# Expert stage of an MoE layer: gather for four experts at a time from a split token-major h

## What is computed

```python
scores = jax.nn.sigmoid((h @ w_router).astype(f32))
...
def expert_block(args):
    e, tok, wr = args
    xb = h[tok]
    y = (jax.nn.silu(xb @ w_gate[e]) * (xb @ w_up[e])) @ w_down[e]
    return y * wr[:, None].astype(h.dtype)
...
shared = (jax.nn.silu(h @ ws_gate) * (h @ ws_up)) @ ws_down
return routed + shared
...
h <- LayerNorm(alpha * h + moe(h))
```

## Time and profile before

| | |
|---|---|
| time, median of 3 runs | 2540.41 us (2539.84 to 2541.12) |
| span of the profiled execution | 2540.7 us, mean granted clock of PE 0.986 |
| PE busy | 2418.9 us (95%) |
| PEld busy | 1855.8 us (73%) |
| DVE busy | 1187.0 us (47%) |
| ACT busy | 676.3 us (27%) |
| POOL busy | 39.4 us (2%) |
| DMA | 635.25 MB, mean 250 GB/s |
| chain that ended last | PE 88%; DVE 8%; issue 2% |

### The profile page before, as it was taken

How to read it: one execution, slowest core, us unless ns; L and a number is a source line. 1 busy time by engine, 2 the same in 40 slices (tenths; PEclk the granted TensorE clock), 3 DMA queues, 4 the chain that set the end, 5 groups by cost and what they waited for, 6 DMA issues and landing times.

```text
span 2540.7 us, 41313 instructions
## 1 busy us (share of the span) xinstructions
PE 2418.9 (95%) x16502; PEld 1855.8 (73%) x16502; DVE 1187.0 (47%) x1447; ACT 676.3 (27%) x719; POOL 39.4 (2%) x36
## 2 busy tenths in 40 slices
PE   6999999999989999999987999999999999999995
PEld 6999999998989999999987544455444445444542
DVE  4346665757654444444456333333233333333335
ACT  3333433333333333333322111111111111111111
POOL 0000000001010000000000000000000000000000
PEclk9999999999999999999998999999999999999998
DMA  4544444443445555555762788898888889888882
GB/s 186 183 160 148 158 144 147 146 162 117 150 160 177 185 186 183 180 185 182 287 252 83 323 361 360 361 380 371 361 359 360 360 367 385 359 361 361 359 361 93
DMA packets 89095, 635.25 MB, mean 250 GB/s; under 512 B 10416, under 2 KB 10544, under 8 KB 12224
## 3 DMA queue, kind: packets, MB, share of 16 engines
q1 hardware_dynamic: 85680, 616.82, 62.0%
q10 hardware_dynamic: 2304, 10.49, 1.0%
q0 software_dynamic: 1040, 6.85, 0.7%
HBM read 632.02 MB, written 2.10 MB: 250 GB/s over the span
## 4 chain that ended last, share of the span: by engine, by line
PE 88%; DVE 8%; issue 2%; ACT 1%; DMA 0%; DVEq 0%; ACTq 0%; SPq 0%
PE bank L240 44%; PE bank L740 17%; PE bank L713 10%; PE bank L763 9%; PE bank L725 4%; PE bank L451 3%; DVE acc L1469 3%; DVE wlo L1007 1%; PE bank L410 1%; ACT whi L784 1%; DVE cv L1103 0%; DMA raw<-units 0%; DVE bns L1324 0%; PE bank L755 0%; DVE ylo L1264 0%
## 5 line engine op out<-in xcount | busy, mean ns | idle before, releaser
L1007 DVE TENSOR_TENSOR wlo<-raw,whi 128x2048 fp32r<-128x2048 f32 x206 | 477.3, 2318 | 460.7 <-ACT whi L784 458.7
L240 PE MATMUL bank<-xhi,whi 128*128 128x256 f32 x1920 | 551.7, 287 | 8.0 <-DVE wlo L1007 8.0
L240 PE MATMUL bank<-xlo,whi 128*128 128x256 f32 x1920 | 544.3, 284 | 0.0
L240 PE MATMUL bank<-xhi,wlo 128*128 128x256 f32 x1920 | 544.3, 283 | 0.0
L784 ACT ACTIVATE whi<-raw 128x2048 fp32r<-128x2048 f32 x204 | 389.6, 1910 | 438.3 <-PE bank L240 438.3
L740 PE MATMUL bank<-wgu,xg 128*64 128x512 f32 x2048 | 445.0, 592 | 1.1 <-DVE xg L1461 1.1
L240 PEld LDWEIGHTS bank<-xhi,whi 128*128 128x128 f32 x1920 | 369.5, 192 | 11.2 <-DVE wlo L1007 9.1
L240 PEld LDWEIGHTS bank<-xlo,whi 128*128 128x128 f32 x1920 | 369.6, 193 | 2.1 <-issue 1.9
L240 PEld LDWEIGHTS bank<-xhi,wlo 128*128 128x128 f32 x1920 | 369.5, 192 | 0.0
L740 PEld LDWEIGHTS bank<-wgu,xg 128*64 128x64 f32 x2048 | 148.0, 137 | 292.2 <-issue 292.2
L713 PEld LDWEIGHTS bank<-pick,h 128*128 128x128 f32 x2112 | 240.8, 194 | 30.5 <-issue 30.5
(11 more groups left out here) (322 smaller groups left out, 2814.8 us busy)
## 6 DMA issues: line engine op xcount, KB each, us to landing
wgu<-wgu SPq DMA_DIRECT2D x248, 1024.0 KB, 14.5
raw<-units SPq DMA_DIRECT2D x210, 1024.0 KB, 4.8
wd<-wd SPq DMA_DIRECT2D x128, 1024.0 KB, 8.6
wgu<-wgu ACTq DMA_DIRECT2D x8, 1024.0 KB, 9.3
h<-xtok POOLq DMA_DIRECT2D x2, 1024.0 KB, 7.0
ln_gain<-lnp POOLq DMA_DIRECT2D x2, 1024.0 KB, 13.0
ln_bias<-lnp POOLq DMA_DIRECT2D x2, 1024.0 KB, 17.9
out<-acc SPq DMA_DIRECT2D x4, 512.0 KB, 2.6
```

What stands on the lines that cost most here:

```text
L240: m = nc.tensor.matmul(out_bank[:, t * UC:(t + 1) * UC], lhsT, rhs, start=first and t == 0 and k == 0 and j == 0, stop=last and k == UK - ...
L1007: V.tensor_tensor(wlo[u % SPLIT][:, :], raw[u % RAW][:, :], whi[u % SPLIT][:, :].bitcast(f32), ALU.subtract).then_inc(lo_done, 1)
```

## The change

`htok` is split, once, into `tok_hi` (ACT, two copies of 128x2048) and `tok_lo` (POOL, two subtractions of 128x2048, written over `htok`). ACT makes ALPHA times h first, straight into `acc`, so that DVE's start of `acc` becomes a plain addition. `pick` now covers four experts (a quad): 128 x 2 x 256, type fp32r. A gather block makes two column blocks of h for four experts, hi and lo, as eight fp32r matmuls with 256 moving columns; eight such blocks make a quad. `xg` is 16 KB wide and doubled, and four blocks for the next quad are done in each pair. They stand between the scatter's parts: block, two chunks, three times, the transposes of `eact`, block, two chunks. The down product uses banks 4, 5, 0 and 1. The loop is unrolled over four pairs. `acc` becomes two tiles, and most small tiles move. Gain and bias of the second LayerNorm are loaded by SP behind the last gate and up product.

DVE does `choose` for a quad and `weigh` (the former pickw pair) at the end of the pair's code; PE waits for `pick_ok` ahead of the gate and up products of each even pair (`half == 0`).

The diff, cut to its core (`...` marks what is left out; ACT's loop mirrors DVE's):

```diff
+QUADS = PAIRS // 2
+Q4 = 4 * CAP
...
-    acc = at("acc", 128, [P, TT, D])
-
-    EP = E + 4
+    acc = [at("acc0", 32, [P, D]), at("acc1", 192, [P, D])]
+    tok_hi = at("h_tok_hi", 128, [P, TT, D], f32r)
+    tok_lo = at("h_tok_lo", 144, [P, TT, D], f32r)
+
+    EP = E + 8
...
-    xg = at("xg", 32, [P, KT, 2 * CAP])
-    pick = at("pick", 56, [P, TT, 2, CAP])
-    pickw = at("pickw", 57, [P, TT, 2, CAP])
+    xg = [at(f"xg{j}", 40 + 16 * j, [P, KT, Q4]) for j in range(2)]
+    pick = at("pick", 200, [P, TT, 4, CAP], f32r)
+    pickw = at("pickw", 202, [P, TT, 2, CAP])
...
+        sp.wait_ge(ex["gu_free"], n_rounds * (4 * PAIRS) + START)
+        sp.dma_start(lng[1][:, :], lnp[2].partition_broadcast(P)).then_inc(ex["g2"], 16)
+        sp.dma_start(lnb[1][:, :], lnp[3].partition_broadcast(P)).then_inc(ex["g2"], 16)
         for t in range(TT):
...
-        pool.wait_ge(unit_used, N_UNITS - N_X)
-        pool.dma_start(lng[1][:, :], lnp[2].partition_broadcast(P)).then_inc(ex["g2"], 16)
-        pool.dma_start(lnb[1][:, :], lnp[3].partition_broadcast(P)).then_inc(ex["g2"], 16)
+        for t in range(TT):
+            pool.wait_ge(tk["alpha_ok"], TT)
+            pool.wait_ge(tk["hi_ok"], t + 1)
+            nc.gpsimd.tensor_tensor(tok_lo[:, t, :], htok[:, t, :], tok_hi[:, t, :].bitcast(f32), ALU.subtract)\
+                .then_inc(tk["lo_ok"], 1)
...
+            pe.wait_ge(tk["lo_ok"], TT)
+
+            def gather_block(i, j, before):
+
+                pe.wait_ge(ex[("xg_act", "xg_dve")[j % 2]], b * (2 * PAIRS + 4) + before + START)
+                for k in range(2):
+                    o = bank[j % 2][:, k * Q4:(k + 1) * Q4]
+                    sl = slice((2 * i + k) * P, (2 * i + k + 1) * P)
+                    for t in range(TT):
+                        for x, h in enumerate((tok_hi, tok_lo)):
+                            mi = nc.tensor.matmul(o, h[:, t, sl], pick[:, t, :, :].rearrange("p j s -> p (j s)"),
+                                                  start=t == 0 and x == 0, stop=t == TT - 1 and x == 1)
+                mi.then_inc(ex["ga_ps"], 1)
...
+                for j in chunks:
+                    t, c = j // 4, j % 4
+                    pe.wait_ge(ex["acc_ok"], b * (8 * PAIRS + 8) + i * 8 + max(0, j - 1) + START)
...
+            pe.wait_ge(ex["pick_ok"], b * (QUADS + 2) + 1)
+            for j in range(8):
+                gather_block(j, j, j // 2)
+            with pe.Fori(0, PAIRS // 4) as four:
+                for u in range(4):
+                    pair = four * 4 + u
+                    it = b * PAIRS + pair
+                    buf, half = xg[u // 2], u % 2
...
+                    if half == 0:
+                        pe.wait_ge(ex["xg_act"], b * (2 * PAIRS + 4) + (pair * 2 + 4) + START)
+                        pe.wait_ge(ex["xg_dve"], b * (2 * PAIRS + 4) + (pair * 2 + 4) + START)
+                        pe.wait_ge(ex["pick_ok"], b * (QUADS + 2) + (four * 2 + (u // 2 + 2)))
+                    pe.wait_ge(ex["a_ok"], it + START)
                     for c in range(4):
...
-            gather(0)
-            with pe.Fori(0, PAIRS) as pair:
-                it = b * PAIRS + pair
-
-                pe.wait_ge(ex["xg_act"], b * (2 * PAIRS + 2) + (pair * 2 + 2) + START)
-                pe.wait_ge(ex["xg_dve"], b * (2 * PAIRS + 2) + (pair * 2 + 2) + START)
-                pe.wait_ge(ex["a_ok"], it + START)
-                for c in range(4):
...
-                gather(pair + 1)
-                pe.wait_ge(ex["a_ok"], it + 1 + START)
-                pe.wait_ge(ex["pt_ok"], it + START)
...
-                pe.wait_ge(ex["y_split"], it * 4 + START)
-                scatter(pair)
-                pe.wait_ge(ex["pickw_ok"], it + 1)
-                pe.wait_ge(ex["at_ok"], it + 1)
...
-                for c in range(4):
-                    pe.wait_ge(ex["y_split"], it * 4 + max(0, c - 1) + START)
...
+                    pe.wait_ge(ex["zero"], b * 3 + 3)
+                    pe.wait_ge(ex["y_split"], it * 4 + START)
+                    pe.wait_ge(ex["pt_ok"], it + START)
+                    for j in range(3):
+                        gather_block(4 * half + j, j, pair * 2 + (4 + j // 2))
+                        scatter(pair, (2 * j, 2 * j + 1))
+                    pe.wait_ge(ex["a_ok"], it + 1 + START)
...
+                    gather_block(4 * half + 3, 3, pair * 2 + 5)
+                    scatter(pair, (6, 7))
+
+                    pe.wait_ge(ex["at_ok"], it + 1)
+                    pe.wait_ge(ex["pickw_ok"], b * (PAIRS + 1) + (pair + 1))
...
+                    for c in range(4):
+                        if c == 2:
+                            pe.wait_ge(ex["xg_act"], b * (2 * PAIRS + 4) + (pair * 2 + 6) + START)
+                        if c == 3:
+                            pe.wait_ge(ex["xg_dve"], b * (2 * PAIRS + 4) + (pair * 2 + 6) + START)
+                        for f in range(2):
+                            pe.wait_ge(d_full[f], it * 32 + 32)
+                            for j in range(2):
+                                mi = nc.tensor.matmul(bank[(4, 5, 0, 1)[c]][CAP * j:CAP * j + CAP, :],
...
+        act.wait_ge(og["scaled_ok"], 4 * TT)
+        nc.scalar.activation(acc[1][:, :], htok[:, 1, :], ACT.Copy, scale=ALPHA).then_inc(tk["alpha_ok"], 1)
...
+        act.wait_ge(lo_done, N_D0)
+        nc.scalar.activation(acc[0][:, :], htok[:, 0, :], ACT.Copy, scale=ALPHA).then_inc(tk["alpha_ok"], 1)
...
+        act.wait_ge(unit_used, N_D0 - N_X)
+        for t in range(TT):
+            nc.scalar.activation(tok_hi[:, t, :], htok[:, t, :], ACT.Copy).then_inc(tk["hi_ok"], 1)
...
-                V.scalar_tensor_tensor(acc[:, t, sl], htok[:, t, sl], ALPHA, bank[2 + i % 5][:, :], ALU.mult, ALU.add)\
-                    .then_inc(sh["acc_ok"], 1)
+                dve.wait_ge(tk["alpha_ok"], TT)
+                V.tensor_tensor(acc[t][:, sl], acc[t][:, sl], bank[2 + i % 5][:, :], ALU.add).then_inc(sh["acc_ok"], 1)
...
+                r = rank[:, :, bass.ds(g * 4, 4)].unsqueeze(3).broadcast_to([P, TT, 4, CAP])
+                sl = slots[:, :].unsqueeze(1).unsqueeze(1).broadcast_to([P, TT, 4, CAP])
+                V.tensor_tensor(pick[:, :, :, :], sl, r, ALU.is_equal).then_inc(ex["pick_ok"], 1)
...
             choose(0)
-            gathered(0, b * PAIRS)
-            choose(1)
+            dve.wait_ge(ex["pt_ps"], b * PAIRS + START)
+            weigh(0)
             V.memset(yehi[:, :].bitcast(f32), 0.0).then_inc(ex["zero"], 1)
             V.memset(yelo[:, :].bitcast(f32), 0.0).then_inc(ex["zero"], 1)
             V.memset(pickT[:, :, :].bitcast(f32), 0.0).then_inc(ex["zero"], 1)
+            for j in range(1, 8, 2):
+                gathered(0, j, j)
+            choose(1)
...
-                r = rank[:, :, bass.ds(pair * 2, 2)].unsqueeze(3).broadcast_to([P, TT, 2, CAP])
-                V.tensor_tensor(pickw[:, :, :, :], sl, r, ALU.is_equal).then_inc(ex["round_end"], 1)
-                gathered(pair + 1, it + 1)
-                choose(pair + 2)
-                dve.wait_ge(ex["acc_ok"], b * (8 * PAIRS + 8) + pair * 8 + START)
-                add_out(pair)
...
+                    dve.wait_ge(ex["acc_ok"], b * (8 * PAIRS + 8) + pair * 8 + START)
+                    add_out(pair, (0, 1))
+                    gathered(buf, 4 * half + 1, pair * 4 + 9)
+                    add_out(pair, (2, 3, 4, 5))
+                    gathered(buf, 4 * half + 3, pair * 4 + 11)
+                    add_out(pair, (6, 7))
...
+                    weigh(pair + 1)
+                    if half == 1:
+                        choose(four * 2 + (u // 2 + 2))
```

228 lines of the change are left out of this document (107 added, 121 removed).

## The result

The changed kernel takes 2438.48 us (median of 4 runs, 2437.67 to 2438.98); the kernel before took 2540.5 beside it. The ratio is 0.9597, with a 95% interval of 0.9583 to 0.961: 4% faster.

The account below looks back on a forecast made before the run. PE was taken as the bound, the DMA engines close behind. Loop start 1416.8 + 32 x 28.9 pairs + 49.5 wait + 25.5 clock + 31.8 + 0.5 end = 2448.9, so 2448.5 us; range 2408 to 2478.

Parts of the forecast that it names:

- The gather: PE's gather in each pair: 32 fp32r matmuls at 0.12 us, 3.84 us for 7.25, a gain of 3.41.
- The scatter: Scatter between gather blocks: PE no longer waits for DVE's additions, 3.76 us for 5.94, a gain of 2.18 a pair.
- The four banks: Down product in four banks: removes waits that already cost almost nothing, taken as 0.
- The new wait: PE's wait for `pick_ok` ahead of gate and up in even pairs: 3.3 us late, 15 times, +49.5 us.
- The clock: PE's granted clock after the new waits: most bring a low-level piece costing 1.7 us, 15 times, +25.5 us.
- rival (a): Expert loop: the wait is as forecast but the clock holds, 2423 us; chance 0.24.
- PEclk at about 0.95: Sign in the expert stage's profile: PE's granted clock below 1.00, at about 0.95.
- Ahead of the loop: Before the first gate and up: POOL's subtractions block DVE's router chain, +9.1 us; loop starts at 1416.8.
- The end: After the last down product: 31.8 us to the span's end, plus 0.5 for `weigh` and `choose`.
- The transfers: Weight loads in the loop: 29.7 us a pair at 424 GB/s, below PE's mean pair of 31.2.
- rival (b): Expert loop: no stretch behind the wait, so the transfers set the pace, 2388 us; chance 0.07.
- Rival (d): Expert loop: transfers cannot hold 424 GB/s without their pause and give only 366, 2549 us; chance 0.03.

Follow-up runs that it names:

- e5: The kernel of e1 with the down weights loaded for the first pair only and used for all pairs: 2374.08 us.
- e4: The changed kernel with the scatter in one piece behind the four gather blocks, on PE and DVE: 2529.24 us.
- e8: The changed kernel with the down product back in banks 4 and 5 in turn, with its former waits: 2432.1 us.
- e3: The changed kernel with `choose` ahead of `weigh` at the end of the odd pairs: 2428.85 us.
- e2: The changed kernel with `tok_lo` made by DVE behind its second start of `acc`, instead of by POOL: 2433.53 us.
- e1: The changed kernel with PE's wait for `pick_ok` moved behind gate and up, ahead of the first gather block: 2396.21 us.
- e11: The changed kernel with the gather in f32 from the high part alone, 32 f32 instructions of 256 columns a pair: 2556.94 us.

## Why the prediction was right, and where it was off

**The gather.** 28.93 us from an even to an odd pair, 28.9 forecast, and e5 runs 28.9 throughout. The price of 0.12 us for an instruction, read from the dense product, held inside a block. The four blocks cost 3.98 us a pair all the same, not 3.84, since in two blocks of the four the first instruction holds up the next for 0.20 to 0.23 us (1990.31 to 1990.54; blocks of 0.95 to 1.05 us); the scatter (3.72 for 3.76) and the down product (6.92 for 7.00) made up for it.

**The scatter.** No idle time ahead of chunks; undone (e4) it costs 2.02 us a pair at full clock, where 2.18 was put. What the prediction did not see is that a kernel with its waits can lose 27 us more to the clock; whether the waits are the cause is open.

**The four banks.** Forecast at nothing, measured at 0.08 us a pair.

**The new wait.** Forecast 3.3 us in 15 places, 49.5. By starts it is 3.40 and 3.44 in turn (listed as 3.24 and 3.28 of idle time), 51.3 us in all. All instructions of the chain stood as put: the last `ye_lo` 0.93 us after PE could have started (1973.96 against 1973.03), then 0.67, 0.53, 0.35, and 0.68 for `choose`; only the way to PE was 0.24 instead of 0.1.

**The clock.** This is the term that was mis-sized. I put "most" waits with a piece of 1.7 us, 25.5 in all; it was six waits, 11.8 us. The kinds of pieces were right (3.4 us, and twice that, at half speed), the number was not. The bounds of 0 to 44 held, but they held nearly anything: 11.8 lies about halfway between the forecast and rival (a), which put 0, and that the time came within 10 us of the forecast is in part luck. The sign "PEclk at about 0.95" did not even follow from the prediction's own 15 pieces, which give 0.97; 0.99 was measured. The runs show why the number could not be had from the earlier trace rows: for stretches of 3.2 to 3.4 us it runs from two (e8) to fifteen (e4), and for shorter ones (e3) it was nine.

**Ahead of the loop.** 1417.58, forecast 1416.8. POOL's lock cost 8.7 us, and 9.1 was put; on top, DVE waited 1.29 us for PE's ranks (0.37 in e2, nothing in the kernel before), which I had not seen.

**The end.** 31.1 us from the end of the last down product (2406.1) to that of the span, instead of 32.3: PE's last scatter ran at full clock to its end (granted clock 1.00 from 2406 to 2416), where in the kernel before it fell in the middle of it (0.82 from 2510 to 2520). That outweighs `weigh` and `choose` ahead of the additions.

**The transfers.** Never waited for, at 0.98 share and 406 GB/s, where 0.95 and 400 were put. As the next bound they cost 29.83 us a pair (e1) where 29.7 was put, and rival (b), at 2388, came out at 2396: its last fourth chunk was used 5 us later, and the clock fell in its last scatter. Rival (d), that they could not hold 424 GB/s without a pause, is out: 422 GB/s over 600 us, with one core at work. The Trainium skill, "DMA: Bandwidth & Descriptors", section "Where 436 GB/s comes from", gives its 358 GB/s as half of what two cores share; the same row disagrees with it as a limit for one core at work.

The sum, corrected: 2448.9 + 0.8 (start) + 2.4 (pairs and waits: 15 x (61.26 - 61.1)) - 13.7 (clock) - 1.2 (end) = 2437.2, the span. Against the kernel before: PE's own work in 32 pairs gives 177 us (34.47 - 28.93 each), of which the new wait takes back 51, the clock 12 and the later start 12, which leaves the 102 that were measured.

What stays open: what makes the clock fall after every wait in e4 and in 14 of 15 in e11. In e4 there are short idle stretches in the scatter ahead, but e11 has none, so they are not needed for it. Both have a longer double pair than the changed kernel (65.29 and 67.46 us). That its length decides how many waits are hit would fit e8 too; no run here changes the length alone.

## What to carry to other kernels

Put a wait in front of the instruction that needs it, and not at the head of the block in which that instruction stands: here 14 us of independent matmuls stood behind a wait for an operand that they did not read, and that cost 42 us, where the change had won 102. When a change takes PE's work away, ask at once which transfer is next, and price it by a stretch of the trace at share 1.00: 29.7 us a pair came from 25 us of trace, and 29.83 was measured over the stage. And a short idle stretch of PE has two prices, its own length and a piece of the lower clock that may or may not follow; the first can be worked out, the second only bounded.

## What the runs showed of the hardware that I had not expected

- After idle stretches of PE of 3.23 to 3.28 us the granted clock fell to its lower level in 2, 5, 6, 6 or 7 of 15 cases, in kernels whose double pairs differ by 0.16 us in 61 or not at all; after 2.35 or 2.40 us in 9 of 15. A kernel with less work for PE on the path (four banks instead of two) was thus 6 us slower.
- In e4 (65.29 us a double pair, short idle stretches of 0.18 and 0.31 us in the scatter) the same wait brought a low piece every time, in 13 of 15 cases of twice the length, and 27 us more of clock cost in the loop than in the changed kernel. In e11 (67.46 us, no such stretches) it was 14 of 15. The cause is open.
- An f32 matmul instruction over 256 columns follows the other after 0.216 us (e11), one over 128 columns after 0.113 (7.25 / 64), so half the instructions with twice the columns save next to nothing; in fp32r 256 columns take 0.12.
